# ScalarE's log and exp table set loaded by name ahead of its use, and the norms of two transformer blocks divided anew between TensorE, VectorE and ScalarE

## What is computed

```python
def rms_norm(x, g):
    x32 = x.astype(jnp.float32)
    y = x32 * lax.rsqrt(jnp.mean(x32 * x32, axis=-1, keepdims=True) + EPS)
    return (y * g.astype(jnp.float32)).astype(x.dtype)
...
    for l in range(DEPTH_2):
        mod = c_act @ w_ada[l] + b_ada[l]
        sh1, sc1, gt1, sh2, sc2, gt2 = [m[:, None, :] for m in jnp.split(mod, N_MOD, axis=-1)]
        h = rms_norm(x, g_norm1[l]) * (1.0 + sc1) + sh1
        u = h @ w_in[l] + b_in[l]
        ...
        x = x + gt1 * (merged @ w_out[l])
        h = rms_norm(x, g_norm2[l]) * (1.0 + sc2) + sh2
        up = causal_depthwise_conv(h @ w_up[l], w_conv[l], b_conv[l])
        a, v_ff = jnp.split(up, 2, axis=-1)
        x = x + gt2 * ((jax.nn.silu(a) * v_ff) @ w_down[l])
```

## Time and profile before

| | us |
|---|---|
| median of 3 runs | 3435.17 (3432.92 to 3439.03) |
| the profiled execution | 3427.3 |
| its span | 3425.5 |
| TensorE matmul busy | 3097.4 (90%) |
| VectorE busy | 1119.8 (33%) |
| ScalarE busy | 645.4 (19%) |

### The profile page before, as it was taken

How to read it: one execution, slowest core, us unless ns; L and a number is a source line. 1 busy time by engine, 2 the same in 40 slices (tenths; PEclk the granted TensorE clock), 3 DMA queues, 4 the chain that set the end, 5 groups by cost and what they waited for, 6 DMA issues and landing times.

```text
span 3425.5 us, 31538 instructions
## 1 busy us (share of the span) xinstructions
PE 3097.4 (90%) x12171; PEld 1674.4 (49%) x12171; DVE 1119.8 (33%) x1865; ACT 645.4 (19%) x1148; POOL 193.4 (6%) x234
## 2 busy tenths in 40 slices
PE   4999675688959999978999999999989999999998
PEld 3444345444447877853455444444434554444444
DVE  3355475675741111122331223331023312233300
ACT  2232412100021111113232111110032311111100
POOL 1000011310001111121000000000000000000000
PEclk7999887898969999989999999999999999999999
DMA  6200000575728999972211212222112012222220
GB/s 218 73 26 25 0 1 1 198 288 203 290 88 305 353 355 338 359 248 88 74 50 49 74 49 74 81 89 70 65 44 94 30 49 74 74 74 74 74 72 39
DMA packets 232992, 413.51 MB, mean 121 GB/s; under 512 B 8337, under 2 KB 137917, under 8 KB 232749
## 3 DMA queue, kind: packets, MB, share of 16 engines
q1 hardware_dynamic: 204800, 314.59, 26.7%
q0 software_dynamic: 27552, 96.17, 7.7%
q10 hardware_dynamic: 525, 1.19, 0.1%
HBM read 386.73 MB, written 25.19 MB: 120 GB/s over the span
## 4 chain that ended last, share of the span: by engine, by line
PE 82%; DMA 7%; DVE 4%; issue 4%; ACT 2%; POOL 0%; SPq 0%; ACTq 0%; POOLq 0%; DVEq 0%
PE PSALL L435 50%; PE PSALL L2221 9%; PE PSALL L1547 6%; DMA AR<-idx_rows 3%; PE PSALL L1555 3%; DMA AR<-hn_rows,AR 2%; DMA W<-in_w_branch_b 1%; PE PSALL L405 1%; PE PSALL L1807 1%; PE PSALL L1102 1%; PE PSALL L711 1%; PE PSALL L730 1%; DVE TMP L414 1%; PE PSALL L335 1%; PE PSALL L449 1%
## 5 line engine op out<-in xcount | busy, mean ns | idle before, releaser
L435 PE MATMUL PSALL<-HN,W 128*128 128x512 f32 x2848 | 1271.7, 603 | 45.0 <-DMA W<-in_w_branch_b 28.2
L435 PEld LDWEIGHTS PSALL<-HN,W 128*128 128x128 f32 x2848 | 541.3, 193 | 729.7 <-issue 693.1
L435 PE MATMUL PSALL<-AR,W 128*128 128x512 f32 x752 | 331.8, 598 | 9.0 <-issue 4.5
L2221 PE MATMUL PSALL<-AR,W 128*128 128x512 f32 x704 | 302.5, 592 | 0.0
L1547 PE MATMUL PSALL<-AR,W 128*128 128x128 f32 x2560 | 291.6, 276 | 7.2 <-DVE AR L1588 7.0
L1547 PEld LDWEIGHTS PSALL<-AR,W 128*128 128x128 f32 x2560 | 288.6, 193 | 10.4 <-issue 10.4
L435 PEld LDWEIGHTS PSALL<-AR,W 128*128 128x128 f32 x752 | 142.7, 191 | 187.5 <-issue 181.0
L2221 PEld LDWEIGHTS PSALL<-AR,W 128*128 128x128 f32 x704 | 133.8, 190 | 168.4 <-issue 168.4
L2199 DVE TENSOR_SCALAR AR<-AR,VEC 128x512 f32<-128x512 f32 x88 | 42.9, 488 | 390.2 <-ACT AR L2179 390.2
L526 DVE TENSOR_TENSOR H<-H,TMP 128x512 f32<-128x512 f32 x40 | 27.7, 692 | 411.2 <-ACT TMP L511 411.2
L2179 ACT ACTIVATE AR<-PSALL 128x512 f32<-128x512 f32 x88 | 52.6, 598 | 533.4 <-PE PSALL L435 533.4
(11 more groups left out here) (447 smaller groups left out, 2696.4 us busy)
## 6 DMA issues: line engine op xcount, KB each, us to landing
W<-in_w_up SPq DMA_DIRECT2D x84, 1024.0 KB
W<-in_w_in SPq DMA_DIRECT2D x26, 2048.0 KB
AR<-in_w_ada POOLq DMA_DIRECT2D x24, 2048.0 KB, 8.2
W<-in_w_gate SPq DMA_DIRECT2D x40, 1024.0 KB
W<-in_w_down SPq DMA_DIRECT2D x40, 1024.0 KB
y_rows<-AR SPq DMA_DIRECT2D x40, 512.0 KB, 10.7
AR<-in_ada_w POOLq DMA_DIRECT2D x8, 2048.0 KB, 8.8
W<-in_w_down SPq DMA_DIRECT2D x8, 2048.0 KB
```

What stands on the lines that cost most here:

```text
L435: mm = pe.matmul(o, l, r, start=(i == 0), stop=(i == len(products) - 1))
L2221: mm = pe.matmul(PS[g % 4][:, :], w[:, k - k0, m * P:(m + 1) * P], FF[:, k, :], start=(k == 0), stop=(k == FT - 1))
```

## The change

**Table sets.** `preload_act_table_set("natural_log_exp_and_others")` is put at the head of `norm_act`, `ml_gates_act`, `ml_post_act` and `gdn_post_act`, ahead of the waits inside them, and in the layers ahead of the squares of both residuals. With that set at hand the compiler places no load between Ln and Exp. Silu's set is loaded at the start of `setup_act`, Sigmoid's at the end of `gdn_post_act` and the head of `branch_act`.

**Shift.** VectorE only writes TMP; ScalarE adds the shift, as an Identity activation with a bias, into HN (`shift_act`), in all six norms that have a shift. The two hand over through `hn_scaled` and `hn_ready`.

**Residuals of the layers.** VectorE reads the finished group from PSUM, times the gate, plus H, in one instruction (`residual_sums_dve`). ScalarE only squares (`residual_squares_act`), behind both residuals of a layer, so that the norm at the head of the next trip of the loop has its squares made at the end of the trip before; for the first layer they are made ahead of the loop. VectorE adds the squares of tiles 0 to 5 into RSTD as they come; TensorE makes three products with ones in place of eight (`summed_norm_pe`): of the sum, and of the squares 6 and 7. The last trip makes such squares too, for a norm that nobody reads.

```diff
+        LN_EXP = "natural_log_exp_and_others"
         def setup_act(act):
+            act.preload_act_table(ACT.Silu)
...
+        SUMS_PER = KC - 3
+        def square_act(act, k, c, summed=None):
             if c >= 2:
-                act.wait_ge(ss_done, k * KC + c - 1)
+                if summed is None:
+                    act.wait_ge(ss_done, k * KC + c - 1)
+                else:
+                    act.wait_ge(sq_summed, summed * SUMS_PER + max(1, c - 2))
             act.activation(SQ[:, c % 2, :], H[:, c, :], ACT.Square).then_inc(sq_ready, 1)
+        def square_sum_dve(dve, k, summed, c):
+            dve.wait_ge(sq_ready, k * KC + c + 1)
+            if c >= 2:
+                dve.wait_ge(sq_summed, summed * SUMS_PER + c - 1)
+            dve.tensor_tensor(RSTD[:, :], SQ[:, 0, :] if c == 1 else RSTD[:, :], SQ[:, c % 2, :], ALU.add).then_inc(sq_summed, 1)
+        def summed_norm_pe(pe, k, summed):
+            pe.wait_ge(sq_summed, summed * SUMS_PER + SUMS_PER)
+            pe.matmul(PS[6][:, :], ones, RSTD[:, :], start=True, stop=False)
+            for c in (KC - 2, KC - 1):
+                pe.wait_ge(sq_ready, k * KC + c + 1)
+                mm = pe.matmul(PS[6][:, :], ones, SQ[:, c % 2, :], start=False, stop=(c == KC - 1))
+            mm.then_inc(ss_done, 1)
         def norm_act(act, own, k):
+            act.preload_act_table_set(LN_EXP)
             for c in range(KC):
                 square_act(act, k, c)
...
-                own(dve.scalar_tensor_tensor(TMP[:, c % 2, :], H[:, c, :], GAIN[:, j, c:c + 1], RSTD[:, :],
-                                             ALU.mult, ALU.mult))
+                if c >= 2:
+                    dve.wait_ge(hn_ready, s + c - 1)
+                dve.scalar_tensor_tensor(TMP[:, c % 2, :], H[:, c, :], GAIN[:, j, c:c + 1], RSTD[:, :],
+                                         ALU.mult, ALU.mult).then_inc(hn_scaled, 1)
+        def shift_act(act, n, j):
+            for c in range(KC):
                 sh = 3 * j * KC + c
-                dve.tensor_scalar(HN[:, c, :], TMP[:, c % 2, :], MOD[:, sh:sh + 1], None, ALU.add).then_inc(hn_ready, 1)
+                act.wait_ge(hn_scaled, n * KC + c + 1)
+                act.activation(HN[:, c, :], TMP[:, c % 2, :], ACT.Identity, bias=MOD[:, sh:sh + 1]).then_inc(hn_ready, 1)
...
+        def residual_squares_act(act, q, norm):
+            for c in range(KC):
+                act.wait_ge(res_added, q * KC + c + 1)
+                square_act(act, norm, c, norm - 4)
+        def residual_sums_dve(dve, q, g0, it, gate, norm):
+            for c in range(KC):
+                dve.wait_ge(proj_done, it[0] * it[1] + (g0 + c + 1))
+                dve.scalar_tensor_tensor(H[:, c, :], PS[(g0 + c) % 4][:, :], MOD[:, gate + c:gate + c + 1], H[:, c, :],
+                                         ALU.mult, ALU.add).then_inc(res_added, 1)
+                dve.wait_ge(res_added, q * KC + c + 1)
+                dve.sem_inc(proj_taken, 1)
+                if 1 <= c < KC - 2:
+                    square_sum_dve(dve, norm, norm - 4, c)
...
         def ml_gates_act(act, own, between):
+            act.preload_act_table_set(LN_EXP)
             for d in range(2):
...
         def gdn_post_act(act, own):
+            act.preload_act_table_set(LN_EXP)
             act.wait_ge(var_ready, 2)
...
             norm_act(act, own, 2)
+            act.wait_ge(hn_ready, 3 * KC)
+            for c in range(KC):
+                square_act(act, 3, c)
             with act.Fori(0, LAYERS) as L:
...
-                norm_act(act, own, L * 2 + 3)
+                rstd_act(act, own, L * 2 + 4 * KC)
+                shift_act(act, L * 2 + 2, 0)
...
-                residual_act(act, L * 2 + 1, LG + GL["out"], gi, 2 * KC, norm=L * 2 + 4)
-                rstd_act(act, own, L * 2 + 4)
+                act.preload_act_table_set(LN_EXP)
+                residual_squares_act(act, L * 2 + 1, L * 2 + 4)
+                rstd_act(act, own, L * 2 + 4 * KC + 1)
+                shift_act(act, L * 2 + 3, 1)
```

More of the change, by code:

```diff
@@ L385, in ada_late_pe, with rstd_act @@
                 ada_block_pe(pe, ADA_FIRST + i)
-        def square_act(act, k, c):
+        SUMS_PER = KC - 3
+        def square_act(act, k, c, summed=None):
             if c >= 2:
-                act.wait_ge(ss_done, k * KC + c - 1)
+                if summed is None:
+                    act.wait_ge(ss_done, k * KC + c - 1)
+                else:
+                    act.wait_ge(sq_summed, summed * SUMS_PER + max(1, c - 2))
             act.activation(SQ[:, c % 2, :], H[:, c, :], ACT.Square).then_inc(sq_ready, 1)
-        def rstd_act(act, own, k):
-            act.wait_ge(ss_done, k * KC + KC)
+        def square_sum_dve(dve, k, summed, c):
[10 more added lines that the diff above has]
+            mm.then_inc(ss_done, 1)
+        def rstd_act(act, own, done):
+            act.wait_ge(ss_done, done)
             own(act.activation(RSTD[:, :], PS[6][:, :], ACT.Ln, scale=1.0 / D, bias=EPSC[:, 0:1]))
@@ L398, in norm_act @@
         def norm_act(act, own, k):
+            act.preload_act_table_set(LN_EXP)
             for c in range(KC):
                 square_act(act, k, c)
-            rstd_act(act, own, k)
+            rstd_act(act, own, k * KC + KC)
         def square_pe(pe, k, c):
@@ L502, in merge_dve, with residual_act @@
                 dve.tensor_tensor(YT[int(it is not None)][:, c, :], m[:, 0, :], m[:, 1, :], ALU.add).then_inc(merged, 1)
-        def residual_act(act, q, g0, it, gate, norm=None):
+        def residual_act(act, q, g0, it, gate):
             for c in range(KC):
@@ L512, in residual_act @@
                                ).then_inc(proj_taken, 1)
-                if norm is not None and c >= 2:
-                    square_act(act, norm, c - 2)
-            if norm is not None:
-                for c in (KC - 2, KC - 1):
-                    act.wait_ge(res_added, q * KC + c + 1)
-                    square_act(act, norm, c)
+        def residual_squares_act(act, q, norm):
+            for c in range(KC):
+                act.wait_ge(res_added, q * KC + c + 1)
+                square_act(act, norm, c, norm - 4)
         def residual_dve(dve, own, q, g0, it, beside=None):
@@ L535, in out_pe @@
                         beside(pe, 4 * hf + m, True)
-                    if norm is not None and 4 * hf + m >= 3:
-                        square_pe(pe, norm, 4 * hf + m - 3)
             if norm is not None:
-                for c in range(KC - 3, KC):
-                    square_pe(pe, norm, c)
+                summed_norm_pe(pe, norm, norm - 4)
         def pad(i, width):
@@ L2477, in _ @@
                 branch_act(act, L)
-                residual_act(act, L * 2 + 1, LG + GL["out"], gi, 2 * KC, norm=L * 2 + 4)
-                rstd_act(act, own, L * 2 + 4)
+                act.preload_act_table_set(LN_EXP)
+                residual_squares_act(act, L * 2 + 1, L * 2 + 4)
+                rstd_act(act, own, L * 2 + 4 * KC + 1)
+                shift_act(act, L * 2 + 3, 1)
                 up_act(act, L)
-                residual_act(act, L * 2 + 2, LG + GL["down"], gi, 5 * KC)
+                act.preload_act_table_set(LN_EXP)
+                residual_squares_act(act, L * 2 + 2, L * 2 + 5)
             own.leave(LAYERS)
@@ L2489, in _ @@
             gain_dve(dve, own, 0, VEC[:, 0, V_GMIX:V_GMIX + KC])
-            norm_dve(dve, own, 0, 0)
+            norm_dve(dve, 0, 0, 0)
             dve.wait_ge(filled, 9)
@@ L2500, in _ @@
             rope_tables_dve(dve, own)
-            norm_dve(dve, own, 1, 1)
+            norm_dve(dve, 1, KC, 1)
             router_dve(dve, own)
@@ L2513, in _ @@
                     gain_dve(dve, own, j, VEC[:, 0, V2[g]:V2[g] + KC])
-                norm_dve(dve, own, L * 2 + 3, 0)
+                norm_dve(dve, L * 2 + 3, L * 16 + 3 * KC, 0)
                 latent_dve(dve, L)
@@ L2519, in _ @@
                 branch_dve(dve, L)
-                residual_dve(dve, own, L * 2 + 1, LG + GL["out"], gi)
-                norm_dve(dve, own, L * 2 + 4, 1)
+                residual_sums_dve(dve, L * 2 + 1, LG + GL["out"], gi, 2 * KC, L * 2 + 4)
+                norm_dve(dve, L * 2 + 4, L * 16 + 4 * KC, 1)
                 up_dve(dve, own, L)
-                residual_dve(dve, own, L * 2 + 2, LG + GL["down"], gi)
+                residual_sums_dve(dve, L * 2 + 2, LG + GL["down"], gi, 5 * KC, L * 2 + 5)
             own.leave(LAYERS)
```

20 lines of the change are left out of this document (12 added, 8 removed).

## The result

The changed kernel takes 3392.27 us (median of 4 runs, 3389.40 to 3399.61) against 3434.05 for the kernel before (4 runs, 3420.37 to 3439.03). The two medians lie 41.8 us apart. The ratio of the runs is 0.9892, with a 95% interval of 0.9876 to 0.9908, which is 37 us, or 32 to 43. The profiled execution took 3394.0 us, its span 3392.0, 33.5 us less than that of before.

The account below looks back on a forecast made before the run. TensorE was taken as the bound (busy 90% of the span), so other engines' work counts only where it stands still, at the norms. Terms summed to 40.3 us, from the median 3435.2 giving 3395; range 3383 to 3407.

Parts of the forecast that it names:

- Prices: Costs per operation: a table load between Ln and Exp costs 1.3 us, not the skill's 2.66 us with drain.
- The pace: Norms with a shift: a tile each 0.78 us in place of 1.18, gaining 2.6 us each at norms 0 and 1.
- Rival 4: Six norms: slow VectorE-ScalarE hand-overs make the kernel slower, 3441 at 1 us each; chance 0.03.
- Norm 0, the gates and all the unit norms: First block: norm 0 gains 3.9 us, mLSTM gates 2.1, its last norm 1.3, unit norms 5.2, delta rule's gates 1.3.
- The forecast's "0" behind the gates: Delta rule's last norm: 1.3 us less, but the merge's first group waits for weights until 660.09, so gain 0.
- rival 1: First block's 13.8 us up to the delta rule are given back at the merge's wait for weights: 3409; chance 0.08.
- Out projection and norm, both layers: Fewer products with ones, a shorter norm and faster tiles gain 6.7 us per layer, twice 13.4.
- First layer's head: Squares start 2.1 us earlier, Exp's load saves 1.3, moved copies and transposes cost 1.1; 2.6 us gained with tile pace.
- The branch back: Loop's return: squares made at the body's end bring the first product 8.5 us earlier, 9.0 in all; bounds 6 to 11.
- rival 2: Loop's return: TensorE's own branch is laid bare, costing up to 5 us, in part beside ScalarE's: 3399; chance 0.11.
- rival 3: Up projections: the clock stays up after shorter TensorE idle time, 1.7 us less in each layer: 3391.5; chance 0.10.
- The end: After the last group, three products with ones stand ahead of the result's transposes: 1.1 us lost.

## Why the prediction was right, and where it wasn't

The time lies 2.7 us from the forecast, and the mechanism of most terms held. That it came so near is in part luck. The rows of the table that repeat sum to 31.2 and 32.8 us, where the forecast has 40.3; what lies between is in stretches that the change doesn't touch and that scatter by 7 to 10 us. The ratio of the runs, 37 us with 32 to 43, lies between the two.

- **Prices.** A load costs 1.3 us on the chain, not 2.66: shown by the run with the sets alone. The drain that the Trainium skill ("ScalarE: Activation LUTs", section "What ACT_TABLE_LOAD costs") adds did not show: by it, as an estimate, this run would have gained some 30 us, and its interval ends at 21.
- **The pace.** 0.77 us a tile against 0.78 forecast; norms 0 and 1 won 3.0 each by it, less 0.2 for the later first tile, against 2.6 forecast, and the up projections won 0.6. At the two heads of the layers the forecast's 0.5 each did not come: the first eight weights there take 9.1 to 9.3 us, before 9.2; behind the second layer's head the grant is 0.50 for the first four microseconds, where it was 0.57. Rival 4 fell with the run that put the shift back.
- **First block.** Norm 0, the gates and all the unit norms came within 0.3 us of their terms. Norm 1's load did cost 1.3 ahead of the first square (3.27 us from TensorE's product before it, in place of 1.99) and saved it ahead of Exp. The forecast's "0" behind the gates was wrong by 2.2 to 2.7 us, which are given back up to the merge. 1.1 to 1.4 of them are rival 1 in small: the load ahead of Exp is gone, and the merge's first product waits that much longer for its weights, as the earlier trace rows let one expect. The other 1.1 lies in the delta rule's first 36 us, with the lower grant shown above.
- **Out projection and norm, both layers.** 13.4 forecast. From the first out group to the up projection it is 60.9 us in place of 67.0 in both layers and all four traces, 6.1, and 0.6 comes by the pace: 6.7 each, together 13.4.
- **First layer's head: the step that failed.** Forecast 2.6 won (2.1 to the first product), measured 1.1 to 2.2 lost. I summed what ScalarE and VectorE do and forgot what a moved step is moved past. TensorE's eight products of the head now stand ahead of the credit for SyncE's load, and the load needs 8 us. Moving the credit gave 3.4 back; against the kernel before the head then wins 1.0 to 1.2, so about 1 us of the 2.1 is still missing, and where is not settled.
- **The branch back: mis-sized.** 9.0 forecast (8.5 of it to the first product), 7.0 to 7.4 measured to the first product, and nothing behind it. I put ScalarE's return at 5.1 us behind its last square. It is of that size, but TensorE's comes later: its last product with ones waits for that last square, ends 1.2 us behind it, and only then does TensorE branch, 4.88 us. That is rival 2, at 1.1 to 1.2 us by the run with TensorE's loop alone written out, and not up to 5. With TensorE's branch away, ScalarE's 5.35 and VectorE's 6.09 stand behind it, so the forecast's 5.1 was right for its own engine.
- **Credit for the move.** The forecast counted the head's squares as what the branch back gains by. Undone, they cost 4.0 there and give 2.1 to 3.0 elsewhere.
- **The clock** (rival 3) stayed up in some executions at some norms, not as a rule.
- **The end** cost 1.0, forecast 1.1.
- **The base.** I set the sum against the median, since the traced execution lay 7.9 us below it. The second traced execution of the kernel before is 4.1 us longer than the first: 6.7 longer in the mLSTM, 3.2 shorter in the router and experts. Set against the first traced execution alone, the forecast would have been 3387.0, below every run.
- **The signs named.** Two of them did not hold. The merge's first group was to start some 13 us earlier than 660.09; it starts at 650.45, 9.6 us earlier, since the delta rule gave 2.2 back and the mLSTM lost 1.4 to its clock (in the second pair of traces it is 17.8 us). And ScalarE's first copy of VEC was to come 2 to 5 us behind its last square; it comes 6.6 us behind (2464.70 to 2471.26), for TensorE's branch. The up projection's 5.85 us against 5.7, the pace, and TensorE's idle time behind the branch (4.88 and 3.38) were as said.

The terms that failed sum to 5.3 to 6.8 us (head 3.7 to 4.8, branch back 1.6 to 2.0, each with its 0.5 of pace), and the delta rule's 2.2 to 2.7 come on top.

## What to carry to other kernels

When a step is moved ahead of a loop on one engine, look at what that engine gives out behind it: a credit for a load that comes late can cost up to the load's whole latency (here 3.4 us of 8). A branch back cost each engine 5 to 7 us from its own last instruction, side by side; it is on the path when the engines have nothing queued, and here it paid only to take all of them away. And where the stretch of interest repeats to the tenth while the whole scatters by 10 us, read the gain at the place, in two traces of each kernel, and keep the whole time for the sum.

## What the runs showed of the hardware

- Naming a table set that was already there loaded it again, 1.28 us, and the load took over the wait of the instruction behind it (norm 2 with the set named twice). Where the load stood ahead of the wait it cost nothing.
- A return to a loop's head cost TensorE 4.7 to 4.9, VectorE 6.1 to 7.1 and ScalarE 5.35 us, where nothing was queued ahead of it.
- With identical work and no idle time, the granted clock differs between executions (0.90 and 1.00 over 34 us in the mLSTM); one kernel's mLSTM took 210.0 and 216.7 us. Behind 3 us of idle time ahead of the up projection the clock fell in 14 of 16 cases, behind 0.4 to 0.5 us in none of four.
